# Latent norms: the place of squares and sums, and the zero products ahead of them

## What is computed

```python
def rmsnorm(x, g):
    xf = x.astype(jnp.float32)
    y = xf * lax.rsqrt(jnp.mean(xf * xf, axis=-1, keepdims=True) + NORM_EPS)
    return (y * g.astype(jnp.float32)).astype(x.dtype)

def mla_mixer(hx, hc, w_in, g_q, w_q, g_kv, w_kv, w_out, with_ctx_out):
    ...
    cq_x, ckv_x, kr_x, gate_x = jnp.split(hx @ w_in, split_at, axis=-1)   # 512, 256, 64, 1024
    q_x = queries(cq_x, True)            # (rmsnorm(cq, g_q) @ w_q), rope on 64 of 192
    k_x, v_x = keys_values(ckv_x, kr_x, True)   # (rmsnorm(ckv, g_kv) @ w_kv), rope on kr
    ...
    return (o_x.reshape(b, n, A_WIDTH) * jax.nn.silu(gate_x)) @ w_out, y_c
```

## Time and profile before

| | us |
|---|---|
| median of three runs | 3299.04 |
| lowest and highest of them | 3296.72, 3301.99 |
| profiled execution, device time | 3295.2 |
| its span, first to last instruction | 3293.4 |
| PE busy in the span | 3028.2 (92%) |
| DVE busy | 1838.2 (56%) |
| ACT busy | 1188.4 (36%) |
| mean granted PE clock, share of full | 0.965 |

### The profile page before, as it was taken

The page is one execution under the profiler, slowest core; times in us unless marked ns, Lnnn a source line. Parts: engine busy times, 40 slices in busy tenths (PEclk is TensorE's granted clock), DMA queues, the critical chain, the costliest instruction groups (busy, mean ns, idle before and its releaser), DMA issues.

```text
span 3293.4 us, 36177 instructions
## 1 busy us (share of the span) xinstructions
PE 3028.2 (92%) x14524; PEld 2386.0 (72%) x14524; DVE 1838.2 (56%) x3248; ACT 1188.4 (36%) x2079; POOL 93.7 (3%) x176
## 2 busy tenths in 40 slices
PE   7999889999999999889998888999998877999997
PEld 5767658778887887777886666788875556777776
DVE  5446678876774574443635555474535667445434
ACT  3234242232223434334534444452322111454443
POOL 0000000100001000000100000011000000000000
PEclk9999989999999998999999899999998998999999
DMA  5222216645554220002220000233322210312002
GB/s 224 96 83 84 71 58 220 227 142 171 166 180 159 87 96 26 13 1 96 84 58 14 13 7 1 96 106 110 112 65 61 61 61 24 124 65 71 20 1 90
DMA packets 102880, 283.53 MB, mean 86 GB/s; under 512 B 16758, under 2 KB 34455, under 8 KB 102456
## 3 DMA queue, kind: packets, MB, share of 16 engines
q1 hardware_dynamic: 91448, 243.80, 22.4%
q0 software_dynamic: 9392, 32.48, 2.7%
q10 hardware_dynamic: 1872, 4.93, 0.4%
HBM read 257.05 MB, written 24.12 MB: 85 GB/s over the span
## 4 chain that ended last, share of the span: by engine, by line
PE 82%; DVE 9%; ACT 7%; issue 1%; ACTq 0%; DMA 0%; POOL 0%; SPq 0%; DVEq 0%; POOLq 0%
PE ps L1639 19%; PE ps L1641 19%; PE ps L1640 19%; PE ps L1860 6%; PE ps L1672 3%; PE ps L1847 2%; PE ps L1918 2%; PE ps L1892 2%; PE ps L1934 1%; ACT pt L2193 1%; PE ps L1816 1%; PE ps L1772 1%; PE ps L1881 1%; ACT tmp L2019 1%; PE ps L1835 1%
## 5 line engine op out<-in xcount | busy, mean ns | idle before, releaser
L1639 PE MATMUL ps<-hh,whi 128*128 128x256 f32 (+1 forms) x2424 | 914.9, 377 | 24.8 <-DVE hl L2369 14.4
L1641 PE MATMUL ps<-hh,wlo 128*128 128x256 f32 (+1 forms) x2424 | 871.2, 359 | 0.0
L1640 PE MATMUL ps<-hl,whi 128*128 128x256 f32 (+1 forms) x2424 | 870.6, 359 | 0.0
L1639 PEld LDWEIGHTS ps<-hh,whi 128*128 128x128 f32 x2424 | 459.2, 189 | 127.3 <-issue 23.5
L1640 PEld LDWEIGHTS ps<-hl,whi 128*128 128x128 f32 x2424 | 460.1, 190 | 90.9 <-issue 20.8
L1641 PEld LDWEIGHTS ps<-hh,wlo 128*128 128x128 f32 x2424 | 458.3, 189 | 71.2
L2378 DVE TENSOR_TENSOR wlo<-raw,whi 128x1024 fp32r<-128x1024 f32 x249 | 304.3, 1223 | 251.5 <-ACT whi L1996 250.9
L1996 ACT ACTIVATE whi<-raw 128x1024 fp32r<-128x1024 f32 x249 | 262.6, 1056 | 322.5 <-PE ps L1641 293.1
L1860 PE MATMUL ps<-pt,v 128*128 128x256 f32 x768 | 225.2, 417 | 15.9 <-ACT pt L2193 15.8
L2193 ACT ACTIVATE pt<-ps 128x512 f32<-128x512 f32 (+1 forms) x200 | 110.0, 579 | 333.6 <-PE ps L1847 333.3
L1860 PEld LDWEIGHTS ps<-pt,v 128*128 128x128 f32 x768 | 136.0, 198 | 59.8 <-ACT pt L2193 32.5
(11 more groups left out here) (357 smaller groups left out, 4696.1 us busy)
## 6 DMA issues: line engine op xcount, KB each, us to landing
raw<-in_wall SPq DMA_DIRECT2D x261, 512.0 KB, 4.1
mb<-in_wmod SPq DMA_DIRECT2D x128, 512.0 KB, 3.6
xb<-xpark SPq DMA_DIRECT2D x24, 384.0 KB, 4.8
xpark<-F POOLq DMA_DIRECT2D x32, 256.0 KB, 2.3
upark<-tmp POOLq DMA_DIRECT2D x18, 384.0 KB, 2.7
u<-upark SPq DMA_DIRECT2D x24, 256.0 KB, 3.0
early<-in_wm SPq DMA_DIRECT2D x8, 512.0 KB, 5.8
early<-in_wmod POOLq DMA_DIRECT2D x8, 512.0 KB, 7.1
```

The costliest lines, as they stand in the source:

```text
L1639: e.matmul(out, L[0], R[0], start=start, stop=False)
L1640: e.matmul(out, L[0], R[1], start=False, stop=False)
L1641: return e.matmul(out, L[1], R[0], start=False, stop=stop)
```

## The change

It touches only `mla` and the table `idle_before`. `latent_norm` is split. `latent_squares` issues the squares as a run of stages of its own, each into its own temporary, right after the last tile that they need was evicted: four after tile 3, two after tile 5. `latent_norm` then holds only the sums, `rstd` and the scaling; for the query latent it stands behind the product of tile 4, for the key and value latent behind the product of the rope key, where it stood behind gate tile 0. The entries of the two query norms leave `idle_before`, and with them 24 zero products.

```diff
-    idle_before = {2: 14, ("lat", 0, 0): 12, ("lat", 3, 0): 12, "out": 9, "head": 10,
+    idle_before = {2: 14, "out": 9, "head": 10,
                    ("tile", True, 0): 17, ("tile", False, 0): 14, ("tile", False, 1): 7}
...
-        def latent_norm(base, nk, segs, width, gain):
+        def latent_squares(base, nk, segs):
             a, b = segs[0][0], segs[-1][1]
-            src = [[(act, ("cq", l, base + k, x)) for x, _ in segs] for k in range(nk)]
-            R = rms_stages(("lat", l, base), CQ[:, base:base + nk], src, a, b, width, nk)
+            t = [tmps.take() for _ in range(nk)]
+            for k in range(nk):
+                stage("square", ("lat", l, base), CQ[:, base:base + nk], [(act, ("cq", l, base + k, x)) for x, _ in segs], k, a, b, t[k])
+            return t
+
+        def latent_norm(base, nk, segs, width, gain, squares):
+            a, b = segs[0][0], segs[-1][1]
+            rid, cs = ("lat", l, base), chunks_of(a, b)
+            bk = [banks.take() for _ in cs]
+            for k in range(nk):
+                stage("sum_squares", rid, k, nk, cs, bk, squares[k])
+                tmps.drop(squares[k])
+            R = tmps.take()
+            stage("rstd", [(rid, a, b, width, cs, bk, R, (pe, ("sq", rid, nk - 1)))])
+            banks.drop(*bk)
             for k in range(nk):
                 stage("latent", l, base + k, a, b, gain[:, k:k + 1], R, ("lat", l, base), segs, [R] if k == nk - 1 else [])
             tmps.drop(R)
...
         play(tile_stages(KD, H, tH, gr, cq(3)))
-        for c in (4, 5):
-            play(tile_stages(KD, H, tH, SEGS, cq(c)))
+        squares = latent_squares(0, 4, gr)
+        play(tile_stages(KD, H, tH, SEGS, cq(4)))
+        latent_norm(0, 4, gr, 512, col("gq", 4 * j, 4), squares)
+        play(tile_stages(KD, H, tH, SEGS, cq(5)))
+        squares = latent_squares(4, 2, SEGS)
         play(tile_stages(KD, H, tH, SEGS, ev_kr))
-        latent_norm(0, 4, gr, 512, col("gq", 4 * j, 4))
+        latent_norm(4, 2, SEGS, 256, col("gkv", 2 * j, 2), squares)
...
         for c in range(8):
             play(tile_stages(KD, H, tH, gr, gate(c)))
-            if c == 0:
-                latent_norm(4, 2, SEGS, 256, col("gkv", 2 * j, 2))
```

## The result

The changed kernel took 3279.88 us (median of five runs, 3272.16 to 3289.41); the kernel before, in five runs beside it, 3299.54 us. The ratio is 0.995 with an interval of 0.9926 to 0.9973. Timed again, the two kernels gave 3280.58 and 3293.94 us, ratio 0.9956 (0.9943 to 0.997). Taken as a ratio of the 3299.04 us that the forecast started from, the result is 3282.5 us, inside the range. The profiled execution after took 3276.62 us with a span of 3274.7 us, 18.7 us less than before.

What follows compares the result with a forecast made beforehand. PE was taken as the bound (82% of the span), with four waits for ACT's squares around the norms. Removing them, 11.0 us in sum, took 3299.0 us to 3288.0 us; the range was 3281 to 3294 us.

Steps and rivals of the forecast that it cites:

- The four waits: PE waits ahead of query and key norm sums, layers 0 and 3: 3.91, 1.84, 3.70, 1.57 us, all removed.
- the four changeovers: PE going from product to sum and back at the four places: 0.5 us either way, zero as value.
- What carries them: At both norms, squares issued early on ACT finish under the next 8.35 us product, so each first sum finds its square done.
- What is pushed back: ACT, DVE and SP work queued later stays hidden; tightest is layer 3's gate tile 2, 2.9 us to spare.
- Rival 1: Late weight slot at gate tile 2, layer 3, perhaps layer 0, returns the key norms' 3.4 us: 3291.4 us; chance 0.08.
- Rival 2: Late squares leave bare waits at the query norms, PE's clock halves: 3315.6 us, slower; chance 0.04.
- rival 3: Attention of layers 0 and 3 reached earlier, low-clock stretches change: 3279 us if gained (0.06), 3297 if lost (0.07).
- The forecast's own sign of rival 3: Layer 0's end of gates to layer 3's latent tiles: traces differ by constant 5.7 us; wandering by whole low stretches shows it.

Runs made afterwards that it cites:

- moved_sums: Changed kernel with sums at the new places but each square issued right ahead of its sum; ratio to the kernel before 1.0012 (0.9999 to 1.0025).
- early_squares: Changed kernel with squares early but both sums back at their old places; ratio to the kernel before 0.9957 (0.9942 to 0.9971).
- before_no_zeros: Kernel before without the 24 zero products ahead of the two query norms, order unchanged; ratio to the kernel before 1.0002 (0.9989 to 1.0015).
- layer 0 only: Changed kernel with the new order in layer 0 alone, layer 3 as before; median 3280.57 us, ratio to the kernel before 0.9962.

## Why the prediction came out as it did

**The four waits: right.** Forecast 11.0 us, measured between marks 11.45 us. The 0.45 us are the four changeovers, for which the forecast allowed 0.5 us either way and took zero: each sum is 0.11 us shorter when PE doesn't stand ahead of it.

**What carries them: right, but told too broadly.** The forecast argued with the square's place in ACT's queue, behind rope copies and Tanh, and took the early squares and the new place of the sums as one. moved_sums shows that the new place of the sums alone gives nothing, early_squares that it is hardly needed.

**What is pushed back: right.** After the rope key of layer 3 the chain to gate tile 2's low part was forecast with 10.8 us and 2.9 us to spare. In the changed kernel DVE's row is

```profile
2938.20 1.22 DVE L2392 TENSOR_TENSOR wlo<-raw,whi 128x1024 fp32r<-128x1024 f32 x1
```

so it ends at 2939.4, 10.7 us after the product's end at 2928.73, and the next product needs it at about 2942.5: 3.1 us to spare. Rival 1 didn't happen. On the table load the rows after agree with those before: Ln ends at 1150.09, the load starts at 1150.16 and Exp at 1151.46, with no drain to be seen.

**Rival 2: not here, but its mechanism is real.** It needed squares later than 8.35 us; they end 3.8 us after tile 3's eviction began. Take the zero products out while the wait is there (before_no_zeros), and the clock falls and the sums take 2.5 and 1.7 us longer. So the forecast's sentence that the zero products are no work that anybody needs was wrong for the old order: they held the clock. Its price for the fall, 20 us of half clock and so 10 us at each of the two norms, was too high. And a late square alone isn't enough: behind bare waits of 1.48 and 1.69 us the sums kept their length, behind those of 3.54 to 3.76 us they didn't.

**The step that fell short: the sum went straight from PE waits to the total.** The forecast's sum has no term for the clock outside the stretches that change, and rival 3 gave that 13% in all. The runs show that it is no rare accident: the clock of one or both attention parts changed in every kernel whose timing was moved, by 3 to 24 us of half clock in a part, worth up to 12 us, as much as the whole change. The forecast's own sign of rival 3 came: the lead of the changed kernel was to stay the same from the end of layer 0's gates to layer 3's latent tiles, and it went from 6.8 to 14.5 us. Moving layer 0 alone gave some 7 us more than its waits, moving layer 3 alone gave its 5.5 us back. Both signs meet in the whole change, since what shifts layer 0's attention out of its long low stretch tends to put low stretches into layer 3's. That the second comparison comes within 2 to 4 us of the forecast gain is in part luck: clock terms of several us each, which the sum left out, partly cancel. The first median, 19.7 us below before, is the 11.45 us and a favourable share of this; the second comparison, with more runs, gives 13.4 us by its medians and 14.5 by its ratio (9.9 to 18.8). Rival 3 named the mechanism, the place (the stretch at 1290 to 1300 of the earlier trace rows) and the time, 3279 us, but it was given too small a chance, and the first median lies 1.1 us below the range, which took only part of it in.

**What stays open.** Why the old timing of layer 0 meets the stretch of 20 us each time, in three profiles of three, while a delay of 1.2 us ends it and one of 2.35 us in the changed kernel doesn't bring it back. The profiles point to the moment at which an attention part starts, but no rule for it was found, and most kernels have one profile only. Why layer 3's part is nearly free of low stretches in both profiles of the kernel before, and in few others, is open too. Whether the average gain really exceeds 11.45 us, by 2 to 3 us, the intervals can't tell.

## What to carry to other kernels

A wait of PE for a producer on a busy in-order engine is removed by issuing the producer's work ahead of whatever else that engine has to do next; moving the consumer isn't enough, and zero products that covered the wait have to go with it, since they are a cost once nothing waits. Where PE works in stretches with waits of 1 to 3 us, a small shift anywhere ahead can be worth as much as the change itself through the granted clock: compare marks around the changed part, not only totals, and give that shift a term of its own in the range. Filling the recurring waits with zero products made the time lower here, by some 8 us, and in six runs of each kernel steadier.

## What the runs showed of the hardware that was not expected

- PE waits of 2.2 to 2.4 us, with products on both sides, can be followed by a stretch of 20 us at 1.2 GHz (PEclk 0.57 over 24 us), or by one of 3.4 us (0.93), with the same work and the same waits: 2.24 us ahead of head 1's first scores both before and after. Nine zero products (2.1 us) in each such wait left one low stretch in layer 0's attention and none in layer 3's.
- Useless work can lower the time: zero products in the attention's waits did, by some 8 us. Five zero products ahead of layer 0's attention took the long low stretch out of the profile, with a median 6 us lower, though the interval of the ratio (0.9977 to 1.0006) still holds 1.
- Bare waits of 3.54 to 3.76 us ahead of the sums made them 1.4 to 2.75 us longer, those of 0.64 to 1.69 us did not, beyond the 0.11 us of a start from a standing PE.
- Executions of one kernel differ by up to 21.7 us (layer 0 only, 3274.87 to 3296.57), those of the changed kernel by 18.8, and its two profiles by 11 us in span, which the clock in the two attention parts accounts for.
